# Turning the delta rule's queries, keys and beta-scaled keys by 32x32 blocks and a broadcast row instead of on TensorE

## The reference

```python
qkv = jax.nn.silu(causal_depthwise_conv(qkv, dn_conv_w))
q, k, v = jnp.split(qkv, 3, axis=-1)
q = l2_normalize(q.reshape(hd))
k = l2_normalize(k.reshape(hd))
beta = jax.nn.sigmoid(b_raw.astype(jnp.float32))
...
q = q * (Dk ** -0.5)
g = jnp.cumsum(g, axis=-1)
k_beta = k * beta[..., None]
a = jnp.einsum("bhncd,bhnsd->bhncs", k_beta, k) * decay
t_mat = jnp.eye(C, dtype=jnp.float32) + jnp.where(strict, a, 0.0)
...
attn = jnp.einsum("bhncd,bhnsd->bhncs", q, k) * decay
```

## Time and profile before

| | |
|---|---|
| median of 3 runs | 2506.94 us (2506.9 to 2507.11) |
| the profiled execution's own time | 2506.8 us |
| its span | 2505.0 us |
| TensorE busy | 2490.8 us, 99% |
| VectorE, ScalarE, GpSimd busy | 1488.8, 1072.3, 104.7 us |
| mean granted clock | 0.999 |
| HBM read and written | 188 GB/s over the span |

### The profile page before, as it was taken

How to read it: one execution, slowest core, us unless ns; L and a number is a source line. 1 busy time by engine, 2 the same in 40 slices (tenths; PEclk the granted TensorE clock), 3 DMA queues, 4 the chain that set the end, 5 groups by cost and what they waited for, 6 DMA issues and landing times.

```text
span 2505.0 us, 28359 instructions
## 1 busy us (share of the span) xinstructions
PE 2490.8 (99%) x11953; PEld 2060.6 (82%) x11953; DVE 1488.8 (59%) x1275; ACT 1072.3 (43%) x883; POOL 104.7 (4%) x178
## 2 busy tenths in 40 slices
PE   9999999999999999999999999999999999999998
PEld 7888888888888888888888888877888888888887
DVE  5465655544456545678779996644655544456544
ACT  5444443333334334555454544533443433333333
POOL 0000000000000000122000002000000000000000
PEclk9999999999999999999999999999999999999999
DMA  8654666665566666787654457743766665566653
GB/s 301 208 187 137 210 227 211 210 210 193 196 215 221 226 195 208 216 288 204 204 167 146 162 189 237 227 144 128 219 217 218 219 198 189 198 203 233 222 198 134
DMA packets 160110, 508.16 MB, mean 203 GB/s; under 512 B 16128, under 2 KB 43920, under 8 KB 158704
## 3 DMA queue, kind: packets, MB, share of 16 engines
q1 hardware_dynamic: 153696, 485.35, 59.6%
q0 software_dynamic: 5872, 20.47, 2.6%
q10 hardware_dynamic: 416, 0.52, 0.1%
HBM read 466.43 MB, written 4.20 MB: 188 GB/s over the span
## 4 chain that ended last, share of the span: by engine, by line
PE 97%; DVE 1%; ACT 1%; DMA 0%; issue 0%; SPq 0%; POOLq 0%; POOL 0%; ACTq 0%
PE ps L840 31%; PE ps L841 30%; PE ps L844 30%; PE ps L1290 1%; PE ps L1306 1%; DVE weights_lo L1836 0%; PE ps L810 0%; DVE conv_out L2117 0%; PE ps L979 0%; DMA weights_raw<-in_w_in 0%; PE ps L1077 0%; PE ps L1050 0%; PE ps L1223 0%; PE ps L1211 0%; PE ps L873 0%; PE ps L862 0%
## 5 line engine op out<-in xcount | busy, mean ns | idle before, releaser
L1836 DVE TENSOR_TENSOR weights_lo<-weights_raw,weights_hi 128x2048 fp32r<-128x2048 f32 x431 | 986.3, 2289 | 883.0 <-ACT weights_hi L1370 883.0
L1370 ACT ACTIVATE weights_hi<-weights_raw 128x2048 fp32r<-128x2048 f32 x431 | 825.2, 1916 | 1172.7 <-PE ps L844 1121.9
L840 PE MATMUL ps<-weights_hi,stationary_hi 128*128 128x512 f32 x2408 | 944.6, 392 | 2.5 <-ACT stationary_hi L1387 1.2
L841 PE MATMUL ps<-weights_lo,stationary_hi 128*128 128x512 f32 x2408 | 937.3, 389 | 0.0
L844 PE MATMUL ps<-weights_hi,stationary_lo 128*128 128x512 f32 x2408 | 741.5, 389 | 0.0
L840 PEld LDWEIGHTS ps<-weights_hi,stationary_hi 128*128 128x128 f32 x2408 | 452.1, 188 | 98.6 <-issue 3.3
L844 PEld LDWEIGHTS ps<-weights_hi,stationary_lo 128*128 128x128 f32 x2408 | 452.0, 188 | 94.4
L841 PEld LDWEIGHTS ps<-weights_lo,stationary_hi 128*128 128x128 f32 x2408 | 452.2, 188 | 92.6 <-issue 0.5
L840 PE MATMUL ps<-weights_hi,hidden_hi 128*128 128x512 f32 x1008 | 392.1, 389 | 0.0
L841 PE MATMUL ps<-weights_lo,hidden_hi 128*128 128x512 f32 x1008 | 392.1, 389 | 0.0
L844 PE MATMUL ps<-weights_hi,hidden_lo 128*128 128x512 f32 x1008 | 310.2, 389 | 0.0
(11 more groups left out here) (351 smaller groups left out, 933.5 us busy)
## 6 DMA issues: line engine op xcount, KB each, us to landing
weights_raw<-in_w SPq DMA_DIRECT2D x128, 1024.0 KB, 5.5
weights_raw<-in_w_in SPq DMA_DIRECT2D x79, 1024.0 KB, 5.6
weights_raw<-in_w_up SPq DMA_DIRECT2D x64, 1024.0 KB, 5.0
weights_raw<-in_w_down SPq DMA_DIRECT2D x64, 1024.0 KB, 5.6
weights_raw<-in_w_out SPq DMA_DIRECT2D x32, 1024.0 KB, 5.7
hidden<-turned_blocks SPq DMA_DIRECT2D x328, 64.0 KB, 2.8
weights_raw<-in_wk SPq DMA_DIRECT2D x16, 1024.0 KB, 5.6
weights_raw<-in_wv SPq DMA_DIRECT2D x16, 1024.0 KB, 5.5
```

What stands on the lines that cost most here:

```text
L840: pe.matmul(o, xh, WHI[:, slot, j, c * BANK:(c + 1) * BANK], start=first and j == 0, stop=False)
L841: pe.matmul(o, xh, WLO[:, low, j, c * BANK:(c + 1) * BANK], start=False, stop=False)
L1370: act.activation(WHI[:, s % NSPLIT], RAW[:, s % NRAW], ACT.Copy).then_inc(hi_ready, 1)
L1836: dve.tensor_tensor(WLO[:, s % NRAW], RAW[:, s % NRAW], WHI[:, s % NSPLIT].bitcast(F32), ALU.subtract).then_inc(lo_ready, 1)
```

## The change

Three operands of the gram and the convolved keys are no longer turned on TensorE.

- Convolved keys: `turn_back` on TensorE goes; a set of moves "bk" does it by blocks, behind "cv" on both queues, and `back_store` copies it into `KTOK`. The sum of squares of the keys moves from z's index 7 to index 4, and their normalisation from ga's index 1 to z's index 7.
- Keys and queries: the sets "nk" and "nq", turned by VectorE at ga's index 0 and 2, moved, and copied by ScalarE from SBUF instead of PSUM. "nq" uses the same buffers as "nk".
- Beta times keys: TensorE turns beta (16 rows) beside the cumulated gate; both rows go to the scratch in DRAM; GpSimd broadcasts beta to all partitions in two DMAs of 512 KB into `KBT`; VectorE multiplies that by the turned keys at ga's index 3. The product in rows (`KB_`) goes.
- The decay matrix's broadcast now waits until queries have been turned by blocks and both broadcasts of beta have landed.
- TensorE's waits for the queries', keys' and convolved keys' transposes go with them; before the gram it waits for the two copies and the product.

```diff
+        RT_BK, RS_BK = back_blocks("turned_k", A0 + 56), back_blocks("hidden_k", A0 + 16)
+        RT_N, RS_N = at("turned_heads", [P, TT, COLS], A0 + 48), at("hidden_heads", [P, TT, P // SIDE, COLS // P, SIDE], A0 + 56)
...
-        scratch = nc.dram_tensor("gate_scratch", (U16, P), F32, kind="Internal").ap()
+        scratch = nc.dram_tensor("gate_scratch", (U16, 2 * P), F32, kind="Internal").ap()
...
-            for n, name in enumerate(("cq", "ck", "cv", "bv"), 1):
-                load_pass(S_IN2 + n * PS, w_in2, IN2_COLS[n], 0, 5, lambda: move_by_sp(sp, name))
+            for n, names in enumerate((["cq"], ["ck"], ["cv", "bk"]), 1):
+                load_pass(S_IN2 + n * PS, w_in2, IN2_COLS[n], 0, 5, lambda: [move_by_sp(sp, name) for name in names])
+            for k in range(PS):
+                load_pass(S_IN2 + 4 * PS + k, w_in2, IN2_COLS[4], k, steps=1)
+                if k >= 5:
+                    move_by_sp(sp, ("nk", "bv", "nq")[k - 5])
...
             move_by_pool(pool, "cv")
+            move_by_pool(pool, "bk")
...
+            move_by_pool(pool, "nk")
             move_by_pool(pool, "bv")
-            pool.wait_ge(qk2_turned, 1)
             pool.wait_ge(gates_landed, 48)
-            pool.dma_start(DEC[:], scratch.partition_broadcast(P)).then_inc(gates_landed, 16)
+            for t in range(TT):
+                pool.dma_start(KBT[:, :, t * P:(t + 1) * P], scratch[t * HEADS:(t + 1) * HEADS, P:].partition_broadcast(P)).then_inc(gates_landed, 16)
+
+            pool.wait_ge(blocks_turned, turns("nq"))
+            pool.wait_ge(gates_landed, 80)
+            pool.dma_start(DEC[:], scratch[:, 0:P].partition_broadcast(P)).then_inc(gates_landed, 16)
+            move_by_pool(pool, "nq")
...
-                    turn_back(COUT, 0, conv_back)
...
-                if k == 2:
+                if k == 6:
                     left(P_IN2 + 3)
-                    pe.wait_ge(qn_ready, 1)
-                    turn_rows(lambda h, t: QTOK[:, t, h * HD:(h + 1) * HD], 1, qk2_turned)
-                elif k == 3:
-                    pe.wait_ge(qk2_ready, 1)
-                    pe.wait_ge(kn_ready, 1)
-                    turn_rows(lambda h, t: KTOK[:, t, h * HD:(h + 1) * HD], 1, qk2_turned)
-                elif k == 4:
                     pe.wait_ge(qk2_ready, 2)
                     pe.wait_ge(kb_ready, 1)
-                    turn_rows(lambda h, t: KB_[:, t, h, :], 1, qk2_turned)
...
-                if k in (2, 3, 4):
-                    act.wait_ge(qk2_turned, k - 1)
-                    dst = (QT2, KT2[:], KBT)[k - 2]
-                    act.activation(dst.rearrange("p h t -> p (h t)"), flat_high, ACT.Copy).then_inc(qk2_ready, 1)
+                if k in (2, 4):
+                    wait_landed(act, ("nk", "nq")[k // 4])
+                    act.activation((KT2[:], QT2)[k // 4].rearrange("p h (j r) -> p h j r", r=SIDE), RS_N[:].rearrange("p t i m r -> p m (t i) r"), ACT.Copy).then_inc(qk2_ready, 1)
...
+                    if k == 4:
+                        back_store(1, KTOK)
                     conv4_tap(2, k - 3)
+                    if k == 4:
+                        sum_squares(1)
...
                 if k == 0:
-                    turn_conv("bv", 2)
-                    dve.wait_ge(l2_ready, 1)
+                    dve.wait_ge(l2_sum, 2)
+                    dve.wait_ge(kn_ready, 1)
+                    turn("nk", KTOK, P_IN2 + 1)
                     dve.tensor_tensor(heads(QTOK), heads(QTOK), l2_of(0), ALU.mult).then_inc(qn_ready, 1)
                 elif k == 1:
-                    dve.tensor_tensor(heads(KTOK), heads(KTOK), l2_of(1), ALU.mult).then_inc(kn_ready, 1)
+                    turn_conv("bv", 2)
                 elif k == 2:
-                    dve.wait_ge(kn_ready, 1)
-                    dve.tensor_tensor(KB_[:], heads(KTOK), per_head(beta[:]), ALU.mult).then_inc(kb_ready, 1)
+                    dve.wait_ge(qn_ready, 1)
+                    turn("nq", QTOK, P_IN2)
                 elif k == 3:
+                    dve.wait_ge(gates_landed, 80)
+                    dve.wait_ge(qk2_ready, 1)
+                    dve.tensor_tensor(KBT, KBT, KT2[:], ALU.mult).then_inc(kb_ready, 1)
                     back_store(2, VTOK)
```

78 lines of the change are left out of this document (31 added, 47 removed).

## The result

| | before | after |
|---|---|---|
| median of the runs, us | 2506.92 (2506.13 to 2507.11, 4 runs) | 2518.91 (2514.99 to 2521.68, 4 runs) |
| profiled execution, us | 2506.8, span 2505.0 | 2519.38, span 2517.6 |

The ratio is 1.0047, 95% interval 1.0035 to 1.0059: slower by 12 us. The forecast was 2512.9, the range 2499.8 to 2519, with 0.44 on slower.

What follows compares the result with a forecast made beforehand. TensorE, busy 99% of the span, was taken to bound the kernel: 2506.8 less 6.9 of removed work plus 12.9 of waits gives 2512.8, or 2512.9 against the median. The range was 2499.8 to 2519.

Steps and rivals of the forecast that it cites:

- rival 3: Clock falls in the wait before ga5: one step 5.45 us longer, 2518.4; chance 0.09, shared with more contention.
- its upper case: Slower landings after "bk", of beta's broadcast and of the queries: waits of 21.5 us in all, 2521.5.
- Removed, -6.9: TensorE work gone: four blocks of 16 transposes, 7.0 us, less 0.1 for beta's added transpose.
- z pass, 0.6: TensorE waits 0.6 us for the split of z6, because VectorE stands until "bk" has landed.
- ga4, 1.4: TensorE waits 1.4 us for the split of ga4, behind ScalarE's copy of the keys ("nk").
- ga5, 5.9: TensorE waits 5.9 us for VectorE's split of ga5, behind the product that needs beta's broadcast; largest term.
- Gram, 1.8: TensorE waits 1.8 us before the gram for ScalarE's copy of the queries, moved behind the decay's broadcast.
- After the gram 0.4, ga7 2.8: TensorE waits 0.4 us for the split of ga6, then 2.8 at ga7's turn for VectorE's mask chain.
- The clock, 0 in the sum: The forecast's sum held no term for a fall of TensorE's clock; only rival 3 did.
- Rival 1: All transfers stay hidden, no waits before ga5, the gram or ga7: 2500.0 us; chance 0.20.
- rival 2: Lowest landing times throughout, only ends of the chain show: 4.5 us of waits, 2504.5; chance 0.17.

Runs made afterwards that it cites:

- e8: Kernel before with only the convolved keys turned by blocks, their copies at index 4 ahead of VectorE's taps: 2505.32 us.
- e1: Kernel before with one transpose of 16 left in each of the four blocks and nothing in their place: 2502.01 us.
- e4: Kernel before with convolved keys and keys by blocks, queries on TensorE, beta's broadcast ahead of the keys' moves, waiting copies and product later: 2503.31 us.
- e7: Changed kernel with the queries' moves issued ahead of the decay's broadcast on GpSimd: 2514.31 us.
- e9: Kernel before with one pause of set length, TensorE idle, just ahead of the gram: 2515.75 us.
- e10: Kernel before with the same pause ahead of the gram as e9, filled with 50 transposes on TensorE: 2513.69 us.
- e5: Changed kernel with 100 more transposes on TensorE, meant to fill its waits before ga5 and the gram: 2516.98 us.
- e6: Changed kernel with VectorE's beta product and copy of the values one index later, behind the split of ga5: 2522.69 us.
- e11: All four blocks of transposes gone, with e4's layout: beta's broadcast ahead of the keys' moves, decay's broadcast last: 2513.12 us.
- e12: Changed kernel with queries' moves ahead of the decay's broadcast, product and both copies of the values later, decay's subtraction later: 2515.39 us.
- e3: Changed kernel without beta's two broadcasts, the product multiplying the turned keys by themselves: 2510.93 us.
- e2: Kernel before with only the convolved keys turned by blocks, their copies at index 5, VectorE's behind its taps: 2511.47 us.

## Why the prediction was right, and where it was not

The time, 2518.9, lies inside the range by 0.1 us, and in the class given most (slower, 0.44). It is 6.0 us over the forecast of 2512.9 and outside the forecast's own range (2507 to 2518), in the part of the range that stood there for rival 3 "or more contention still", at 0.09. Two of the four runs lie above the range. So the direction and the mechanism held, and that the median lies within the range is partly luck. The range was also cut short: its upper case was worked out at 2521.5 and the range stopped at 2519. By TensorE's terms, forecast first:

- **Removed, -6.9.** Held roughly: e8 gained 1.5 of 1.76 for one block, e1 4.9 and a wait of 1.3 for 15/16 of four, e4's profiled execution 4.7 of the 5.2 us of three of them, beta's transpose counted (its median 3.6).
- **z pass, 0.6.** None. "bk" was in by 1160.4, not 1162.0, since "cv" was copied 0.9 us sooner; the split of z6 started at 1166.44, not 1168.1.
- **ga4, 1.4.** 1.56.
- **ga5, 5.9.** 8.23. The mechanism is as told: VectorE stood at the product, waiting for beta.
- **Gram, 1.8.** 4.60, behind ScalarE's copy of the queries, as told.
- **After the gram 0.4, ga7 2.8.** 0.0 and about 0.1.
- **The clock, 0 in the sum.** 4.9 us in TensorE's time, 2.1 behind the wait before ga5 and 2.75 in the gram.

The chain that ended last says in fewer numbers where the 6.6 us between the forecast of the profiled execution (2512.8) and its time (2519.4) arose:

| link | forecast | trace |
|---|---|---|
| keys' moves, GpSimd's first issue to their landing | 1187.8 to 1197.1 | 1186.7 to 1197.5 |
| beta's second broadcast, issue to landing | 1202.2 to 1210.7 | 1202.3 to 1212.3 |
| queries' moves, GpSimd's first issue to ScalarE's copy | 1211.8 to 1221.1 | 1214.0 to 1227.8 |
| that copy to the operand of the turn in ga7 | 1221.1 to 1238.1 | 1227.8 to 1244.8 |

The last link is right to 0.1 us. The first is right by two errors that cancel: it began 1.1 us sooner and took 1.5 us longer. The miss is in the other two. Beta's broadcast took 10.0 us and not the 8.5 taken from the decay's row (the upper bound of 12.7 was not reached, though the decay's own broadcast took 13.3), and GpSimd went on 0.5 us later. The queries' moves behind the decay's broadcast took 13.8 us and not 9.3; one of them landed 10.7 us after its issue, where 5.8 was taken. Together the queries came 6.7 us late. e7, which takes the queries out from behind the decay, had no wait before the gram and copied them from 1218.34.

The clock is not the term that was missing. The forecast had its fall as rival 3, an alternative at 5.45 us for one step. It came along with the forecast's waits, twice, but both times inside slack: the 2.1 us shortened the wait before the gram, and the 2.75 stand where the forecast had the wait of 2.8 in ga7. Adding 4.9 to the sum would count that 2.8 twice. The Trainium skill, "TensorE: Matmul & The Clock Gate", section "What's actually happening", says: "the default state is throttled, and activity releases the throttle". The traces agree: 0.50 behind the wait of 4.60, 0.50 behind e9's pause, 1.00 where e10 filled it.

Rival 1 (all hidden) and rival 2 (2504.5) fell: beta's broadcast was not in by 1203. Of what was to show the steps right, all but one stood in the profile: the wait before ga5 behind VectorE's split with the product's DMA wait ahead of it (3 to 9 us were named), the gram's behind ScalarE's copy, and the late loads. SyncE's load of z6 went out at 1157.90 and that of ga7 at 1202.56, some 10 and 6 us after the step that frees the buffer, where 11 and 6 were named; ScalarE waited 1.1 us for the first and TensorE not at all. The wait at the turn in ga7 did not show.

The estimate of 2.2 us for a move of 64 KB, from "DMA: Bandwidth & Descriptors" of the Trainium skill, was met by two sets: the convolved keys, 2.1 us in the median by GpSimd and 2.4 by SyncE, and the values, 2.3 and 2.6. The moves of "nk" took 5.3 and 5.8, those of "nq" 9.8 and 4.1.

What remains open: why the decay's broadcast took 13.3 us here and 9.1 in the executions of e5 and e6, and how much of that, and of the queries' 9.8, is the share of the DMA engines (1.01 between 1209 and 1223 here). No kernel with fewer loads in that stretch was run.

## What to carry to other kernels

- Adding up the busiest engine's waits works only while that engine is what the end waits for. Here a chain of transfers and VectorE's work had taken its place from 1186.7 to 1244.9 us, and a wait or a slow stretch inside that time was not a loss of its own. Follow the chain that ends last, and price its links.
- A fall of the clock behind a wait costs where no later wait absorbs it: about 2 us behind the set pause (e9 against e10). From the start of ga7's turn to the end of the execution it was 1274.5 to 1274.6 us in the traces of the kernel before and of the changed one, and 1276.0 and 1276.1 in those of e7 and e11, where TensorE had waited 2.19 and 3.51 us at that turn.
- Follow one queue's sets of transfers as a chain, each link from first issue to landing (7 to 11 us here for the keys' or the values' 16 moves of 64 KB over two queues, 13.8 for the queries' behind a broadcast), and count how many links stand before the first use. Moving a use later only moved the wait (e6, e12). With beta's broadcast ahead of the keys' moves the wait before ga5 was gone (e11), and with the queries left on TensorE as well, so that their set was not a link, all were (e4).
- A copy that waits for a transfer stands in its engine's list ahead of the next split. Look for the second such copy before removing the first (e3), and put an operand's two halves at places that both engines reach together (e2, e8).
